# Root mean squares of two branches taken in columns by token instead of rows over all partitions, in a decoder layer on one core

## The reference, cut to what matters

```python
def rms_norm(x, g):
    return x * lax.rsqrt(jnp.mean(jnp.square(x), axis=-1, keepdims=True) + NORM_EPS) * g

# SSD branch: 4 groups of 512 channels each
y = (y + d_skip[:, None] * xs).reshape(b, s, SSD_INNER) * jax.nn.silu(z)
y = rms_norm(y.reshape(b, s, SSD_GROUPS, -1), norm_g.reshape(SSD_GROUPS, -1))
# attention branch: 8 heads of 128 channels each
o = rms_norm(o, subln_g) * (1.0 - lam_init)
# both
mixed = (gates[..., :D] * (y @ w_ssd_br) + gates[..., D:] * (o @ w_diff_br)) @ w_mix_out
x = layer_norm(DN_ALPHA * x + mixed, ln1_g, ln1_b)
x = layer_norm(DN_ALPHA * x + memory_cross_attention(x, mem, w_cq, w_ckv, w_co), ln2_g, ln2_b)
```

## Time and profile before

| | |
|---|---|
| median of 3 runs | 1071.47 us (1071.45 to 1071.48) |
| the profiled execution | 1072.56 us, its span 1070.40 us |
| mean granted TensorE clock | 0.995 |
| TensorE matmuls busy | 1040.8 us, 97% |
| VectorE busy | 524.6 us, 49% |
| ScalarE busy | 376.0 us, 35% |
| HBM traffic | 288.78 MB read, 271 GB/s over the span |

### The profile page before, as it was taken

How to read it: one execution, slowest core, us unless ns; L and a number is a source line. 1 busy time by engine, 2 the same in 40 slices (tenths; PEclk the granted TensorE clock), 3 DMA queues, 4 the chain that set the end, 5 groups by cost and what they waited for, 6 DMA issues and landing times.

```text
span 1070.4 us, 16979 instructions
## 1 busy us (share of the span) xinstructions
PE 1040.8 (97%) x6816; PEld 762.5 (71%) x6817; DVE 524.6 (49%) x983; ACT 376.0 (35%) x662; POOL 57.3 (5%) x53
## 2 busy tenths in 40 slices
PE   8999999999999999999999999999999999999995
PEld 7999999999999999999865445545544555445452
DVE  6998456676789966755852222122211222222223
ACT  5655535555675643454311111111111111111112
POOL 0002003243000000000200000000000000000000
PEclk9999999999999999999999999999999999999998
DMA  7664443343443456469589999999985999999912
GB/s 291 210 224 158 158 150 126 126 145 126 148 167 123 154 184 216 157 254 414 195 307 406 417 402 420 382 409 406 415 359 229 398 417 419 414 386 397 415 62 79
DMA packets 41644, 290.72 MB, mean 272 GB/s; under 512 B 4712, under 2 KB 5872, under 8 KB 6896
## 3 DMA queue, kind: packets, MB, share of 16 engines
q1 hardware_dynamic: 40800, 284.62, 68.2%
q0 software_dynamic: 784, 5.24, 1.3%
HBM read 288.78 MB, written 1.06 MB: 271 GB/s over the span
## 4 chain that ended last, share of the span: by engine, by line
PE 85%; DVE 10%; ACT 2%; issue 2%; DMA 1%; SPq 0%; ACTq 0%; DVEq 0%
PE stream L1466 22%; PE stream L1796 21%; PE stream L1822 11%; PE stream L1491 8%; PE stream L1737 6%; PE work L1785 6%; DVE w_lo L949 3%; DVE acc L986 2%; DVE rms L1112 2%; DMA raw<-in_wdense 1%; PE stream L1808 1%; PE work L1592 1%; PE work L1568 1%; PE stream L1815 1%; PE work L1674 1%
## 5 line engine op out<-in xcount | busy, mean ns | idle before, releaser
L949 DVE TENSOR_TENSOR w_lo<-raw,w_hi 128x1024 fp32r<-128x1024 f32 x142 | 171.1, 1224 | 54.0 <-ACT w_hi L657 53.9
L1796 PE MATMUL stream<-ring,xg 128*64 128x512 f32 x640 | 197.2, 593 | 0.2 <-issue 0.2
L657 ACT ACTIVATE w_hi<-raw 128x1024 fp32r<-128x1024 f32 x142 | 147.0, 1051 | 55.0 <-DMA raw<-in_wdense 40.1
L1466 PE MATMUL stream<-xT_hi,w_hi 128*128 128x256 f32 x560 | 160.4, 286 | 1.3 <-DVE w_lo L949 1.3
L1466 PE MATMUL stream<-xT_lo,w_hi 128*128 128x256 f32 x560 | 157.9, 282 | 0.0
L1466 PE MATMUL stream<-xT_hi,w_lo 128*128 128x256 f32 x560 | 157.8, 282 | 0.0
L1796 PEld LDWEIGHTS stream<-ring,xg 128*64 128x64 f32 x640 | 64.7, 137 | 88.8 <-issue 88.8
L1466 PEld LDWEIGHTS stream<-xT_hi,w_hi 128*128 128x128 f32 x560 | 106.1, 189 | 6.1 <-issue 3.5
L1357 DVE TENSOR_TENSOR hh<-h,stream 128x256 f32<-128x256 f32 x32 | 13.5, 422 | 196.9 <-ACT h L878 196.9
L1466 PEld LDWEIGHTS stream<-xT_hi,w_lo 128*128 128x128 f32 x560 | 105.9, 189 | 0.0
L1466 PEld LDWEIGHTS stream<-xT_lo,w_hi 128*128 128x128 f32 x560 | 105.6, 189 | 0.2 <-issue 0.2
(11 more groups left out here) (364 smaller groups left out, 2092.0 us busy)
## 6 DMA issues: line engine op xcount, KB each, us to landing
ring<-in_wstream SPq DMA_DIRECT2D x120, 1024.0 KB, 9.3
raw<-in_wdense SPq DMA_DIRECT2D x73, 1024.0 KB, 4.8
place_e<-in_wstream SPq DMA_DIRECT2D x24, 1024.0 KB, 9.4
place_m<-in_wstream SPq DMA_DIRECT2D x12, 1024.0 KB, 9.0
place_c<-in_wstream SPq DMA_DIRECT2D x12, 1024.0 KB, 10.6
place_w<-in_wstream SPq DMA_DIRECT2D x12, 1024.0 KB, 8.5
place_x<-in_wstream SPq DMA_DIRECT2D x12, 1024.0 KB, 10.1
ln<-in_lnp POOLq DMA_DIRECT2D x3, 1024.0 KB, 7.0
```

Source lines behind the costliest of these rows:

```text
L657: nc.scalar.activation(w_hi[:, q % ROUNDED, :], raw[:, q % 6, :], ACT.Copy).then_inc(w_rounded, 1)
L949: tt(w_lo[:, q % 6, :], raw[:, q % 6, :], w_hi[:, q % ROUNDED, :].bitcast(F32), ALU.subtract).then_inc(w_rest, 1)
L1466: last = mm(S[n % 4][:, 0:SEQ], w[:, b, :], a[:, kb, :], start=(kb + j == 0), stop=(kb == chunks * KB - 1 and j == len(parts) - 1))
L1796: last = mm(S[2][e * SLOTS:(e + 1) * SLOTS, :], x[:, kb, col + e * SLOTS:col + (e + 1) * SLOTS], tiles[e][kb // 4][:, kb % 4 * 512:(kb % 4 ...
```

## The change

The sums of squares are made with tokens on partitions. The squares become the stationary operand and one column of ones the moving one: for attention 8 heads x 2 token blocks, 16 matmuls of one column into 16 columns of `W[0]`; for SSD 4 groups x 2 token blocks x 4 channel blocks, 32 matmuls of one column into 8 columns of `W[1]`. `inverse_rms` scales and inverts 16 or 8 columns of 128 partitions, `root` takes their roots. `spread` brings each column back to all partitions: the column, broadcast to 128x128, is the stationary operand, the identity the moving one with 128 columns, into work banks; 16 such matmuls for attention after ck 5, 8 for SSD after cv 2. DVE multiplies straight from these banks.

ACT takes the first roots behind ck 4 (before: behind ck 7), the second ones behind cv 1 (before: cv 3). DVE's order becomes: `inverse_rms(0)`, rests for ck 5, products of attention, rests for ck 7, rests of oT, `inverse_rms(1)`, rests for cv 1 and cv 3, `scale_y(0)`.

In the layer norms a root of a constant, written to an unused column, stands ahead of the roundings of mix and of co, so that ACT loads the root table there. `normalise_in_two` is split: only the subtraction of the mean stays ahead of mix output 7, the second half of block 0 follows output 7 and its rests. cvb 1 moves ahead of `turn(0)`, on TensorE and in ACT's order of reading.

```diff
-        rms = sb("rms", [P, 8, 512], SL3)
+        rms = sb("rms", [P, 2 * DIFF_HEADS + 2 * GROUPS], SL3)
+        rms_cols = (slice(0, 2 * DIFF_HEADS), slice(2 * DIFF_HEADS, 2 * DIFF_HEADS + 2 * GROUPS))
...
             for g in range(GROUPS):
                 nc.scalar.activation(z[:, 4 * g:4 * g + 4, :], z[:, 4 * g:4 * g + 4, :], ACT.Silu).then_inc(z_silu, 1)
                 leave("ck", g, kcT[:, g, :])
+            def root(branch):
+                cols = rms_cols[branch]
+                act.wait_ge(rms_rcp, branch + 1)
+                nc.scalar.activation(rms[:, cols], rms[:, cols], ACT.Sqrt).then_inc(rms_sqrt, 1)
             for k in range(GROUPS):
                 squares_of_y(k)
                 leave("ck", GROUPS + k, kcT[:, GROUPS + k, :])
-            def root(k):
-                w = 512 if k < GROUPS else SEQ
-                act.wait_ge(rms_rcp, k + 1)
-                nc.scalar.activation(rms[:, k, 0:w], rms[:, k, 0:w], ACT.Sqrt).then_inc(rms_sqrt, 1)
-            for k in range(GROUPS):
-                root(k)
+                if k == 0:
+                    root(0)
             for g in range(2):
                 act.wait_ge(oT_done, 4 * g + 4)
                 nc.scalar.activation(oT_r[0][:, 4 * g:4 * g + 4, :], oT[:, 4 * g:4 * g + 4, :], ACT.Copy
                                      ).then_inc(oT_rounded, 1)
             leave_tokens("cv", 0, vc)
             leave_tokens("cv", 1, vc)
+            root(1)
             leave_tokens("cv", 2, vc)
             leave_tokens("cv", 3, vc)
             act.wait_ge(act_took, taken_count(out_index("gate", 15)))
-            for k in range(GROUPS):
-                root(GROUPS + k)
             for g in (2, 3, 0, 1):
                 nc.scalar.activation(gt[:, 4 * g:4 * g + 4, :], gt[:, 4 * g:4 * g + 4, :], ACT.Sigmoid
                                      ).then_inc(gate_sig, 1)
...
                 act.wait_ge(mix_done, k + 1)
                 nc.scalar.activation(mixT_r[0][:, k, :], mixT[:, k, :], ACT.Copy).then_inc(mixT_rounded, 1)
                 round_chunks(out_index("ssd", k))
+            nc.scalar.activation(exp_alog[:, 0:1], ones[:, 0:1], ACT.Sqrt)
             for k in range(8):
                 round_chunks(out_index("mix", k))
             def norm_sqrt(which):
...
             norm_sqrt(0)
             leave_tokens("cvb", 0, vc, 512)
+            leave_tokens("cvb", 1, vc, 512)
             turned(x1T_r[0], 0)
-            leave_tokens("cvb", 1, vc, 512)
             leave_tokens("cvb", 2, vc, 512, then_round=False)
             turned(x1T_r[0], 1)
             round_chunks(out_index("cvb", 2))
...
                 act.wait_ge(cav_mm, h + 1)
                 nc.scalar.activation(ocT_r[0][:, 2 * h:2 * h + 2, :], W[h][:].rearrange("p (k q) -> p k q", k=2), ACT.Copy
                                      ).then_inc(cav_cp, 1)
+            nc.scalar.activation(exp_alog[:, 0:1], ones[:, 0:1], ACT.Sqrt)
             for k in range(8):
                 round_chunks(out_index("co", k))
             norm_sqrt(1)
...
                    ).then_inc(yz_done, 1)
                 chunk_rests(out_index("ck", g))
-            def mean_squares(k):
-                w, width, factor = (512, P, SUBLN_SCALE ** 2) if k < GROUPS else (SEQ, INNER // GROUPS, 1.0)
-                ve.wait_ge(ssq_mm, k + 1)
-                ts(rms[:, k, 0:w], W[k % 4][:, 0:w], 1.0 / width / factor, EPS / factor, ALU.mult, ALU.add
-                   ).then_inc(ssq_took, 1)
-            def invert(k):
-                w = 512 if k < GROUPS else SEQ
-                ve.wait_ge(ssq_took, k + 1)
-                nc.vector.reciprocal(rms[:, k, 0:w], rms[:, k, 0:w]).then_inc(rms_rcp, 1)
+            def inverse_rms(branch):
+                width, factor = ((P, SUBLN_SCALE ** 2), (INNER // GROUPS, 1.0))[branch]
+                cols = rms_cols[branch]
+                ve.wait_ge(ssq_mm, branch + 1)
+                link(ts(rms[:, cols], W[branch][:, cols], 1.0 / width / factor, EPS / factor, ALU.mult, ALU.add))
+                nc.vector.reciprocal(rms[:, cols], rms[:, cols]).then_inc(rms_rcp, 1)
+            inverse_rms(0)
+            chunk_rests(out_index("ck", 5))
             for k in range(GROUPS):
-                mean_squares(k)
-            for k in range(GROUPS):
-                invert(k)
-                chunk_rests(out_index("ck", 4 + k))
-            for k in range(GROUPS):
-                ve.wait_ge(rms_sqrt, k + 1)
+                ve.wait_ge(rms_mm, k + 1)
                 for j in range(2):
                     h = 2 * k + j
-                    stt(oT[:, h, :], oT[:, h, :], subln, rms[:, k, j * SEQ:(j + 1) * SEQ], ALU.mult, ALU.mult
+                    stt(oT[:, h, :], oT[:, h, :], subln, W[(k + 1) % 4][:, j * SEQ:(j + 1) * SEQ], ALU.mult, ALU.mult
                         ).then_inc(oT_done, 1)
+            chunk_rests(out_index("ck", 7))
             for g in range(2):
                 ve.wait_ge(oT_rounded, g + 1)
                 tt(oT_r[1][:, 4 * g:4 * g + 4, :], oT[:, 4 * g:4 * g + 4, :],
                    oT_r[0][:, 4 * g:4 * g + 4, :].bitcast(F32), ALU.subtract).then_inc(oT_rest, 1)
+            inverse_rms(1)
             chunk_rests(out_index("cv", 1))
-            for k in range(GROUPS):
-                mean_squares(GROUPS + k)
-                invert(GROUPS + k)
             chunk_rests(out_index("cv", 3))
             ve.wait_ge(yz_done, GROUPS)
             def scale_y(g):
-                ve.wait_ge(rms_sqrt, GROUPS + g + 1)
+                ve.wait_ge(rms_mm, GROUPS + g + 1)
                 for b in range(4 * g, 4 * g + 4):
-                    stt(xc[:, b, :], xc[:, b, :], ssd_g[:, b:b + 1], rms[:, GROUPS + g, 0:SEQ], ALU.mult, ALU.mult
-                        ).then_inc(yT_done, 1)
+                    stt(xc[:, b, :], xc[:, b, :], ssd_g[:, b:b + 1], W[2 + g // 2][:, g % 2 * SEQ:(g % 2 + 1) * SEQ],
+                        ALU.mult, ALU.mult).then_inc(yT_done, 1)
             scale_y(0)
...
                 ve.wait_ge(ln_sqrt, TB * which + t + 1)
                 return ts(xres[:, t, :], xres[:, t, :], mv[:, t, 0:1], rstd[:, t:t + 1], ALU.subtract, ALU.mult)
-            def normalise_in_two(t, weights):
+            def subtract_mean(t, weights):
                 link(stt(xres[:, t, :], xres[:, t, :], neg_mean[:, t:t + 1], weights[:, 0, :], ALU.add, ALU.mult))
+            def scale_and_bias(t, weights):
                 ve.wait_ge(ln_sqrt, t + 1)
                 stt(xres[:, t, :], xres[:, t, :], rstd[:, t:t + 1], weights[:, 1, :], ALU.mult, ALU.add
                     ).then_inc(ln_done, 1)
...
             def first_norm_begun():
                 ve.wait_ge(ln_ld, 16)
-                normalise_in_two(0, ln1)
+                subtract_mean(0, ln1)
             def gain_bias(t, weights):
                 link(tt(xres[:, t, :], xres[:, t, :], weights[:, 0, :], ALU.mult))
...
             ve.wait_ge(xres_ld, 16)
             add_output("mix", before_last=first_norm_begun)
-            normalise_in_two(1, ln1)
+            scale_and_bias(0, ln1)
+            subtract_mean(1, ln1)
+            scale_and_bias(1, ln1)
             chunk_rests(out_index("cvb", 0))
             for k in range(4):
                 ve.wait_ge(xt_cp, k + 1)
...
                 mm(W[1][:, P:SEQ], v[:, 1, i * P:(i + 1) * P], attnT[:, SEQ:384], start=False, stop=True,
                    skip_group_check=True).then_inc(av_mm, 1)
-            def sums_of_squares(k):
-                pe.wait_ge(squared, k + 1)
-                if k < GROUPS:
-                    if k == 0:
-                        pe.wait_ge(attnT_cp, 8)
-                        pe.wait_ge(av_cp, 8)
-                        pe.wait_ge(y_done, 8)
-                    last = mm(W[k][:], ones, sqd[:, 2 * k:2 * k + 2, :], start=True, stop=True)
+            def sums_of_squares(branch):
+                if branch == 0:
+                    pe.wait_ge(squared, GROUPS)
+                    pe.wait_ge(attnT_cp, 8)
+                    for h in range(DIFF_HEADS):
+                        for t in range(TB):
+                            last = mm(W[0][:, TB * h + t:TB * h + t + 1], sqd[:, h, t * P:(t + 1) * P], ones[:, 0:1],
+                                      start=True, stop=True)
                 else:
-                    g = k - GROUPS
-                    pe.wait_ge(ssq_took, g + 1)
-                    for j in range(4):
-                        last = mm(W[g][:, 0:SEQ], ones, z[:, 4 * g + j, :], start=(j == 0), stop=(j == 3))
+                    pe.wait_ge(squared, 2 * GROUPS)
+                    pe.wait_ge(oT_done, 2)
+                    for g in range(GROUPS):
+                        for t in range(TB):
+                            c = 2 * DIFF_HEADS + TB * g + t
+                            for j in range(4):
+                                last = mm(W[1][:, c:c + 1], z[:, 4 * g + j, t * P:(t + 1) * P], ones[:, 0:1],
+                                          start=(j == 0), stop=(j == 3))
```

(30 more changed lines are left out.)

## The result

The changed kernel takes 1076.07 us in the median (six runs, 1074.51 to 1076.19); the kernel before, run beside it, 1071.47 (1070.16 to 1071.70). The ratio is 1.0042, 95% interval 1.0032 to 1.0053: slower by 4.6 us, where 2.3 us less had been forecast. The first rival, the falling clock in the sums, had said 1074.7. The profiled execution took 1074.51, with a span of 1072.3 us.

What follows compares the result with a forecast made beforehand. TensorE, busy for 97% of the span, was taken as the bound. Terms -6.1 - 2.2 + 0.4 + 5.5 + 0.1 = -2.3 us took the median 1071.47 to 1069.2 us; term bounds 1068.3 to 1070.4, range 1068.2 to 1076.0.

Steps and rivals of the forecast that it cites:

- The first rival: In the sums, single moving columns let TensorE's clock fall: 3 to 8 us, taken as 5.5, so 1074.7 us; chance 0.26.
- The sums of squares: TensorE's two blocks of sums, 32 and 64 records at 0.112 us: +0.4 us, bounds -0.25 to +2.1.
- The step of 0.133: Diff's matmuls behind the gap start every 0.133 us against 0.118; if of another cause, 1.8 of the 6.1 stays.
- Gap and aftermath in diff: TensorE's wait in diff for VectorE's late rests (2.64 us) and the slow matmuls behind it (3.47) go: -6.1 us.
- The first layer norm: The gap before the first turn shrinks from 2.50 to 0.28 us: gain 2.2 us.
- Spreads: Spreading back on TensorE, 48 records at 0.112 us: 5.4 us, bounds 5.1 to 6.6, plus 0.1 for entering and leaving blocks.
- Root wait: After ck 5 TensorE waits 0 to 0.3 us for ScalarE's first roots, taken as 0.1.
- late first root: Rival: a table load holding ScalarE twice its 1.28 us makes TensorE wait 1.3 us longer after ck 5: 1070.5; chance 0.02.
- VectorE no longer late: Without the reciprocals, VectorE's rest for diff output 2 is ready near 349.5, 3 us early.
- new gap: Late loads or roundings at ssd or cq priced at 0, upper end 0.5; small-waits rival 1070 to 1072, chance 0.15.
- it does not do what it says: Rival: the diff gap stays because ScalarE's roundings or a late tile replace VectorE: +3.8 us, 1075.3; chance 0.07.

Runs made afterwards that it cites:

- experiment 1: The changed kernel with 128 columns of ones moving in both blocks of sums in place of one: 1069.86 us, ratio 0.9985.
- Experiment 7: The kernel before with all reciprocals cut to 16 columns in place of 512 and 256, so its output differs: 1067.58 us, ratio 0.9959.
- experiment 8: The kernel before, unchanged, run and profiled once more: 1071.51 us, the profiled execution 1071.50.
- experiments 5: The kernel before with the layer-norm part of the change alone, sums and reciprocals untouched: 1068.06 us, ratio 0.9969.
- experiment 9: The kernel before with one line added, the root table loaded ahead of the first norm: 1069.07 us, ratio 0.9978.
- experiments 6: The changed kernel with its layer-norm part taken back, leaving the root-mean-square part alone: 1079.76 us, ratio 1.0069.
- experiments 3: The changed kernel with 128 columns of ones moving in the first block of sums only, the second keeping single columns: 1074.51 us.
- experiment 2: The changed kernel with 128 columns of ones moving in the second block of sums only, the first keeping single columns: 1071.54 us.
- experiment 4: The changed kernel with the second block of sums cut into 32 records behind ck 6 and 32 behind ck 7: 1076.08 us, ratio 1.0048.

## Why the prediction was wrong, point by point

**The sums of squares: the step that failed.** It priced 48 matmuls at 0.112 us a record, +0.4, with bounds from -0.25 to +2.1, all at full clock. The price of a record at full clock was right: 0.109 in the first block (3.49 us for 32), 0.110 in the second where 128 columns move (7.06 for 64). What failed is that the bounds left the clock out and gave it to a rival at 0.26. Measured, this term is +6.4 in place of +0.4: 0.2 at full clock (3.49 and 7.06, against 3.43 and 6.90 before) and the 6.2 that lie between experiment 1 and the changed kernel. The argument "each record loads 128 columns of weights and TensorE is never idle" is true of the trace and did not carry: the stretch stands as busy, 7.00 of 7.00 us, and the clock was 0.50 in it.

**The rival was right in place and price.** It said 3 to 8 us, taken as 5.5: nearly all in the second block (+3 for doubled loads, +1.7 behind), in the first once or not at all. The trace has +3.36 in the block (10.42 against 7.06) and 3.2 us at half rate behind it, and the runs give 4.65 for the second block and 0, 1.6 or 3 for the first, where the rival had at most one fall of 1.7. The step of 0.133 that it had as part of its upper bound did not come. The two places that bore on it (2.76 us without a matmul, with a fall behind them, and 2.6 us without one, with none) show an idle engine, and no row of before has a block like this one. With nothing in the trace on either side, 0.26 against 0.50 was too sure. The Trainium skill ("TensorE: Matmul & The Clock Gate", Part 4) has transposes not counting as busy in the same way, which pointed to this rival; experiment 1 shows the like for one-column matmuls, worth 6.2 us here.

**Gap and aftermath in diff, -6.1: right for the profiled execution, too large by 2.1 for the median.** Experiment 7 has 6.10 from profile to profile and 4.0 between medians; against the profile of experiment 8 it has 4.06. Of the three parts, the gap (2.64) stood in all four profiled executions with VectorE's queue as before (experiments 5, 8, 9); the half rate in three of the four; the step of 0.133 for 16 us only in the one of the earlier trace rows, with a milder form of it in experiment 9 (144 matmuls in 17.5 us, 0.122 each). So the 1.8 of the step belongs to that execution. The prediction took the difference from the trace and hung it on the median, which lay 1.1 lower; an execution above its median can hold something that the median lacks, and the step was that here. What the step comes from stays open: the gap and the half rate stood without it in experiments 5 and 8.

**The first layer norm, -2.2: right in the trace, more in the median.** From the first matmul of ssd to that of the expert loop the kernel before takes 176.60 us (369.67 to 546.27), the changed one 174.08 (374.31 to 548.39): -2.5. The turn starts at 0.59 behind the last matmul of cvb 1, a gap of 0.47 where 0.28 was worked out. The medians give more, 3.6 (experiment 5). What fits the rest is that in some executions the clock fell behind the old gap, as the profiles of experiments 6 and 8 show (those of the earlier trace rows and of experiment 7 do not). The prediction had used that gap as evidence that 2.6 us without a matmul bring no fall. It was one execution.

**Spreads, +5.4 and 0.1 for entering: right.** 3.59 and 1.71, 5.30 together, at full clock.

**Root wait, +0.1: 0.28, within its 0 to 0.3, and no late first root.** ScalarE behind ck 4, then TensorE's last matmul of ck 5:

```profile
315.62 1.28 ACT L774 ACT_TABLE_LOAD   x1
316.91 0.22 ACT L774 ACTIVATE rms<-rms 128x16 f32<-128x16 f32 x1
```

```profile
316.78 0.28 PE L1466 MATMUL stream<-memT_hi,w_lo 128*128 128x256 f32 x1
```

The root starts 1.29 us behind the start of the load and is done at 317.13, where 317.0 was forecast. The spreads start at 317.18, 0.40 behind the last matmul of ck 5 where a step is 0.12: TensorE waited 0.28 us for the root. Its last matmul stands as busy until 317.06, so the view of waits does not name this. The drain of about 1.38 us that the Trainium skill ("ScalarE: Activation LUTs", What ACT_TABLE_LOAD costs) adds to a switch is not there.

**VectorE no longer late: right, with less to spare.** Its rests for diff outputs 2 and 3:

```profile
353.16 2.36 DVE L952 TENSOR_TENSOR w_lo<-raw,w_hi 128x1024 fp32r<-128x1024 f32 x2 [5.09 <-ACT w_hi L658]
```

They are done at 355.5; output 2 starts 48 steps of 0.118 behind 351.60, at 357.3, so 1.8 us early, not 3. Five idle microseconds stand ahead of them. No new gap came at ssd or cq. The rival "it does not do what it says" falls.

**The sum.** Experiment 1 is the changed kernel without the falling clock. Its profiled execution took 1069.82, where the profile-to-profile forecast said 1070.3, and its median is 1069.86 against the forecast 1069.2. That the rest of the forecast fits so well is in part luck: between medians the gap in diff was worth 4.0 and not 6.1, the first layer norm 3.6 and not 2.2, and the two errors, of 2.1 and 1.4, go against each other. With the measured terms, -4.0 - 3.6 + 0.2 + 5.3 + 0.3 = -1.8, and experiment 1 lies 1.8 below the kernel before beside it. Of the 6.9 us between 1069.2 and 1076.07, the clock made 6.2.

The same terms say something else. The forecast had the root-mean-square part at -0.1 (-6.1 + 0.4 + 5.5 + 0.1); measured, at full clock it costs 5.8 us (sums, spreads, root wait) and gains 4.0 in diff, a loss of 1.8. Experiment 5, with the layer-norm part alone, is just that much faster than experiment 1 (1068.06 against 1069.86). The falling clock made a bad trade worse; it did not spoil a good one.

## What to carry to other kernels

Price a stretch of TensorE not only by its records but by what moves in them: a block of one-column matmuls with full stationary operands can stand as busy and still end at half clock, and the cure may be free: here 128 columns took no longer a record than one (0.110 against 0.109). Before a term is taken from one profiled execution, look at where that execution lies among the runs; half-rate stretches behind a gap come in some executions and not in others, so in the median a gap can be worth more than its length and less than its worst aftermath. And before moving all work off a late engine, work out how late it is: a gap of 2.64 us was closed by sparing VectorE 7 us of reciprocals, for a third of the spread records. Sum each part of a change by itself as well; here one part earned the whole gain and the other was a loss.

## What the runs showed of the hardware that had not been expected

- Single moving columns with 128x128 f32 stationary operands: the granted clock fell to 0.50 inside a block of 64 records, for 10.2 us, in all four profiled executions that had the block whole (the changed kernel twice, experiments 3 and 6); the same block with 128 moving columns kept 1.00 and took 7.06 us.
- With blocks of 32 such records (3.5 us) the clock fell in some executions and not in others: 0, 1.6 or 3 us by execution in experiment 2, and half-rate stretches of 3.4 and 6.8 us in experiment 4. Cutting a block of 64 in two brought no gain (1076.08 against 1076.07).
- With a 128x128 f32 stationary operand the step of a record hardly depends on what moves: 0.109 with one column, 0.110 with 128 ones, 0.107 to 0.112 for a broadcast column against the identity. That fits the weight load setting the step; no run varies the weight load.
- 2.76 us without a matmul had 3.4 us at half rate behind them in three of four executions; 2.6 to 2.9 us without one, before turn 0, in two of four (experiments 6 and 8, not the earlier trace rows or experiment 7).
- Steps above 0.118 at a granted clock of 1.00 occur in single executions: 0.133 for 16 us in the earlier trace rows, 0.122 on average over diff in experiment 9.
